# Attention stage of a fused two-block kernel: value products of the local heads turned, the two maps of a differential head joined before their transposes

## What is computed

```python
# local ("swa") heads: 8 query heads of 64, 2 key/value heads, window 128, a sink logit each
p = softmax(concat([scores, sink]))[..., :-1]
y_a = rms_norm(einsum("bnhgqk,bnkhd->bnqhgd", p, vv), swa_out_g)          # over all 512 columns
# differential heads: 4 heads, two maps each, values 128 wide
p_diff = p[:, :, 0] - lam * p[:, :, 1]
y_b = rms_norm(einsum("bhqk,bkhe->bqhe", p_diff, v), subln_g) * (1 - lambda_init)   # per head
x = x + rms_norm(concat([y_a, y_b]) @ w_out, attn_post_g)
```

## Time and profile before

| | |
|---|---|
| median of 3 runs | 759.88 us |
| the profiled execution | 760.85 us |
| its span in the profile | 758.9 us |
| TensorE busy | 749.4 us, 99% |
| VectorE, ScalarE, GpSimd busy | 581.2, 447.7, 211.6 us |
| steps 3 to 22 and the rest of `out2` in the profile | about 388 to 479 us |

### The profile page before, as it was taken

The page is one execution under the profiler, slowest core; times in us unless marked ns, Lnnn a source line. Parts: engine busy times, 40 slices in busy tenths (PEclk is TensorE's granted clock), DMA queues, the critical chain, the costliest instruction groups (busy, mean ns, idle before and its releaser), DMA issues.

```text
span 758.9 us, 16885 instructions
## 1 busy us (share of the span) xinstructions
PE 749.4 (99%) x5994; PEld 728.1 (96%) x5994; DVE 581.2 (77%) x1071; ACT 447.7 (59%) x751; POOL 211.6 (28%) x138
## 2 busy tenths in 40 slices
PE   9999999999999999999999999999999999999997
PEld 8999999999999999999999989999999999988885
DVE  5898986768888877435977896799999999973333
ACT  6644455466665665445855666877666666643431
POOL 0477643460000000342563002522122122122220
PEclk9999999999999999999999999999999999999999
DMA  8565554555555567545443333455555555665651
GB/s 293 191 224 193 184 164 134 195 187 200 188 193 187 177 222 250 189 141 187 141 167 111 114 111 112 139 176 198 196 184 189 193 187 180 214 221 189 183 183 55
DMA packets 37919, 135.49 MB, mean 179 GB/s; under 512 B 4465, under 2 KB 4721, under 8 KB 37873
## 3 DMA queue, kind: packets, MB, share of 16 engines
q1 hardware_dynamic: 37728, 134.86, 53.3%
q10 hardware_dynamic: 144, 0.00, 0.0%
HBM read 133.80 MB, written 1.05 MB: 178 GB/s over the span
## 4 chain that ended last, share of the span: by engine, by line
PE 85%; DVE 5%; ACT 4%; issue 3%; POOL 2%; DMA 1%; DVEq 0%; SPq 0%; POOLq 0%; ACTq 0%
PE bank L1852 24%; PE bank L1853 23%; PE bank L1854 23%; PE bank L2295 4%; PE bank L2294 4%; PE bank L2293 4%; DVE w_lo L1168 2%; ACT w_hi L773 2%; POOL X L741 1%; DMA X<-in_x 1%; PE bank L1908 1%; PE bank L2125 1%; PE bank L2145 0%; ACT score L1063 0%; POOL w_lo L622 0%
## 5 line engine op out<-in xcount | busy, mean ns | idle before, releaser
L1852 PE MATMUL bank<-h_hi,w_hi 128*128 128x256 f32 x1372 | 386.1, 281 | 1.1 <-DVE h_lo L1180 1.0
L1853 PE MATMUL bank<-h_lo,w_hi 128*128 128x256 f32 x1372 | 383.0, 279 | 0.0
L1854 PE MATMUL bank<-h_hi,w_lo 128*128 128x256 f32 x1372 | 383.0, 279 | 0.0
L773 ACT ACTIVATE w_hi<-raw 128x1024 fp32r<-128x1024 f32 (+2 forms) x243 | 258.8, 1067 | 89.9 <-PE bank L2295 41.0
L1168 DVE TENSOR_TENSOR w_lo<-raw,w_hi 128x1024 fp32r<-128x1024 f32 (+2 forms) x187 | 236.1, 1264 | 94.3 <-ACT w_hi L773 92.3
L1852 PEld LDWEIGHTS bank<-h_hi,w_hi 128*128 128x128 f32 x1372 | 257.9, 188 | 2.7 <-DVE w_lo L1246 0.8
L1853 PEld LDWEIGHTS bank<-h_lo,w_hi 128*128 128x128 f32 x1372 | 257.9, 188 | 0.0
L1854 PEld LDWEIGHTS bank<-h_hi,w_lo 128*128 128x128 f32 x1372 | 257.8, 188 | 0.0
L622 POOL TENSOR_TENSOR w_lo<-raw,w_hi 128x1024 fp32r<-128x1024 f32 (+1 forms) x56 | 139.0, 2484 | 380.8 <-ACT w_hi L773 372.6
L1226 DVE TENSOR_TENSOR bank<-bank,scales 128x256 f32<-128x256 f32 x116 | 49.5, 430 | 26.2 <-PE bank L1854 17.6
L1507 DVE SCALAR_TENSOR_TENSOR cg<-bank,vec,cg 128x255 f32<-128x255 f32 x108 | 51.3, 475 | 0.7 <-ACT cg L1003 0.6
(11 more groups left out here) (232 smaller groups left out, 978.8 us busy)
## 6 DMA issues: line engine op xcount, KB each, us to landing
raw<-in_w_up SPq DMA_DIRECT2D x108, 512.0 KB, 3.3
raw<-in_w_in SPq DMA_DIRECT2D x53, 512.0 KB, 3.5
raw<-in_w_down SPq DMA_DIRECT2D x32, 512.0 KB, 4.1
raw<-in_w_down SPq DMA_DIRECT2D x16, 704.0 KB, 4.1
raw<-in_w_o SPq DMA_DIRECT2D x8, 512.0 KB, 3.3
raw<-in_w_gate SPq DMA_DIRECT2D x8, 512.0 KB, 3.4
raw<-in_w_out SPq DMA_DIRECT2D x8, 512.0 KB, 3.3
raw<-in_w_b_out SPq DMA_DIRECT2D x4, 512.0 KB, 3.7
```

Source lines behind the costliest of these rows:

```text
L773: nc.scalar.activation(hi_of(u)[:, cols], raw[s][:, cols], ACT.Copy).then_inc(hi_ready, 1)
L1852: nc.tensor.matmul(ps, wh, hi[:, k, :], start=start and n == 0, stop=False)
L1853: nc.tensor.matmul(ps, wh, lo[:, k, :], start=False, stop=False)
L1854: last = nc.tensor.matmul(ps, wl, hi[:, k, :], start=False, stop=stop and n == len(ks) - 1)
```

## The change

1. **Local heads.** Heads are taken in pairs (one of each key/value group) every second step. v is now the stationary operand, 64 columns wide, and `prob_T` streams, 256 columns and then 128. The outputs of the two heads go to partitions 0 to 63 and 64 to 127, feature-major already. The reciprocals are written 64 times over by VectorE (128x2x64), transposed by TensorE (2), copied by ScalarE (`keep_denominators`), and one VectorE multiply scales the pair (`keep_swa`). The 8 transposes of `y_a` go. Its norm is summed over partitions: ScalarE squares (4), GpSimd adds (3), two 128x1 matmuls (`swa_mean_squares`), mean square, power, two transposes to broadcast (`broadcast_swa_rms`), a ScalarE copy, and VectorE applies gain and scale (`swa_source`, 4).
2. **Differential heads.** GpSimd scales the first map (`scale_first`, 2 instructions), VectorE adds the second map times its own factor (`join`, 2), and one set of transposes and value products per head replaces two. The value product stays in PSUM: squares and scaling read it there.
3. **Order.** The transposes of a joined map come in the step of the second map's reciprocals, behind the scores. In the last step the remaining parts of `out2` units 1 to 3 come ahead of the last transposes of y. Rows of `w_out` and of the gain are permuted on the host.

The core of the diff:

```diff
...
-        steps[m + 3]["score"], steps[m + 4]["trans"], steps[m + 5]["pv"] = m, m, m
+        steps[m + 3]["score"], steps[m + 4]["den"] = m, m
+        if m < N_SWA:
+            steps[m + 4]["trans"] = m
+        if m < N_SWA and m % 2 == 1:
+            steps[m + 5]["swa_pv"] = m // 2
+        if m >= N_SWA and m % 2 == 1:
+            h = (m - N_SWA) // 2
+            steps[m + 4]["trans"], steps[m + 5]["pv"] = N_SWA + h, h
         if m % 2 == 0:
             steps[m + 3]["pair"] = m
-    for i in range(5):
-        at = (7 if i == 0 else 7 + 2 * i) + 5
+    steps[13]["swa_stat"], steps[14]["swa_rms"] = True, True
+    steps[15]["swa_chunks"], steps[16]["swa_chunks"] = [0, 1], [2, 3]
+    for i in range(1, 5):
+        at = 12 + 2 * i
         steps[at]["y_sum"], steps[at + 1]["y_scale"] = i, i
-        steps[at + 2]["y_chunks"] = [0, 1] if i == 0 else [3 + i]
-        if i == 0:
-            steps[at + 3]["y_chunks"] = [2, 3]
+        steps[at + 2]["y_chunks"] = [3 + i]
...
+            def scale_first(m):
+
+                pool.wait_ge(den_done, DEN[m])
+                for b, (lo, hi) in enumerate(block_cols(m)):
+                    nc.gpsimd.tensor_scalar(score[:, m % N_SWA, lo:hi], score[:, m % N_SWA, lo:hi],
+                                            rden[:, m, b:b + 1], None, ALU.mult
+                                            ).then_inc(first_scaled, 1)
...
+                if step["swa_pv"]:
+                    p = step["swa_pv"]
+                    pool.wait_ge(swa_sq, p + 1)
+                    if p > 1:
+                        pool.wait_ge(swa_sum_step, p - 1)
+                    nc.gpsimd.tensor_tensor(swa_sum[:], swa_sq_tile[p][:], swa_sum[:], ALU.add
+                                            ).then_inc(swa_sum_step, 1)
+                if step["swa_rms"] or step["y_scale"] is not None:
+                    i = step["y_scale"] or 0
                     pool.wait_ge(y_ms_done, i + 1)
                     nc.gpsimd.tensor_tensor(y_rstd[:, i, :], y_ms[:, i, :], minus_half[:, 0:2],
                                             ALU.pow).then_inc(y_rstd_done, 1)
+                if step["den"] is not None and step["den"] >= N_SWA and step["den"] % 2 == 0:
+                    scale_first(step["den"])
...
+            def keep_denominators(p):
+
+                act.wait_ge(pv_done, 2 * p + 2)
+                nc.scalar.activation(swa_den[p % 2][:], pv_ps[:, TOK:], ACT.Copy).then_inc(den_kept, 1)
...
             def y_squares(i):
-                act.wait_ge(y_done, 2 * (8 if i == 0 else 8 + 2 * i))
+                act.wait_ge(pv_done, N_SWA + i)
                 for b in range(2):
-                    part = y_a[:, b, :] if i == 0 else y_b[:, b, P * (i - 1):P * i]
-                    if 2 * i + b:
-                        act.wait_ge(y_ss_done, 2 * i + b)
+                    part = pv_ps[:, b * P:(b + 1) * P]
...
+                if step["swa_pv"] is not None:
+                    keep_denominators(step["swa_pv"])
                 if step["trans"] is not None:
                     copy_prob_T(step["trans"])
+                if step["swa_pv"] is not None:
+                    swa_square(step["swa_pv"])
...
+                if kind == "swa":
+                    both = rden_swa[m // 2 % 2][:].rearrange("p (b g n) -> p b g n", b=2, g=2)
+                    nc.vector.reciprocal(both[:, :, h // 4, :], row_sum[:, m, :].unsqueeze(2)
+                                         .broadcast_to([P, 2, HD])).then_inc(den_done, 1)
+                    return
...
+            def join(m):
+
                 dve.wait_ge(den_done, DEN[m])
-                for b in range(2):
-                    if kind == "swa":
-                        nc.vector.tensor_scalar(y_a[:, b, HD * h:HD * (h + 1)],
-                                                pv_ps[:, HD * b:HD * (b + 1)],
-                                                rden[:, m, b:b + 1], None, ALU.mult
-                                                ).then_inc(y_done, 1)
-                    else:
-                        y, pv = y_b[:, b, P * h:P * (h + 1)], pv_ps[:, P * b:P * (b + 1)]
-                        if part == 0:
-                            nc.vector.tensor_scalar(y, pv, rden[:, m, b:b + 1], None, ALU.mult
-                                                    ).then_inc(y_done, 1)
-                        else:
-                            dve.wait_ge(y_done, 2 * m)
-                            nc.vector.scalar_tensor_tensor(y, pv, rden[:, m, b:b + 1], y, ALU.mult,
-                                                           ALU.add).then_inc(y_done, 1)
+                dve.wait_ge(first_scaled, m - N_SWA + 1)
+                for b, (lo, hi) in enumerate(block_cols(m)):
+                    second = score[:, m % N_SWA, lo:hi]
+                    nc.vector.scalar_tensor_tensor(second, second, rden[:, m, b:b + 1],
+                                                   score[:, (m - 1) % N_SWA, lo:hi], ALU.mult, ALU.add
+                                                   ).then_inc(diff_joined, 1)
+
+            def keep_swa(p):
+
+                dve.wait_ge(den_kept, p + 1)
+                nc.vector.tensor_tensor(y_a[:, p, :], pv_ps[:, 0:TOK], swa_den[p % 2][:], ALU.mult
+                                        ).then_inc(y_done, 4)
...
+            def swa_mean_square():
+                dve.wait_ge(swa_stat_done, 1)
+                nc.vector.tensor_scalar(y_ms[:, 0, :], bank[slot(IN2_TILE["swa_stat", 0])][:, 0:2],
+                                        D / 512, EPS, ALU.mult, ALU.add).then_inc(y_ms_done, 1)
+
+            def swa_source(c):
+
+                n = CHUNK0["y"] + c
+                dve.wait_ge(swa_scaled, 1)
+                src_free(n)
+                nc.vector.scalar_tensor_tensor(src[n % 2][:], y_a[:, c, :], vcol("swa_out_g_2", c),
+                                               swa_scales[:], ALU.mult, ALU.mult).then_inc(src_ready, 1)
...
+                if step["swa_rms"]:
+                    swa_mean_square()
+                for c in step["swa_chunks"]:
+                    swa_source(c)
                 if n != LATE_STEP:
                     for c in step["y_chunks"]:
                         y_gained(c)
-                if step["trans"] is not None:
-                    denominators(step["trans"])
-                if step["pv"] is not None:
-                    scaled_output(step["pv"])
+                if step["den"] is not None:
+                    denominators(step["den"])
+                if step["den"] is not None and step["den"] >= N_SWA and step["den"] % 2 == 1:
+                    join(step["den"])
+                if step["swa_pv"] is not None:
+                    keep_swa(step["swa_pv"])
...
             def transposes(m):
-                pe.wait_ge(exp_done, 2 * (m + 1))
-                source = pieces(m)
+                if m < N_SWA:
+                    pe.wait_ge(exp_done, 2 * (m + 1))
+                    source = pieces(m)
+                else:
+                    pe.wait_ge(diff_joined, 2 * (m - N_SWA + 1))
+                    source = pieces(2 * m - N_SWA + 1)
...
-            def value_product(m):
-                kind, h, _ = MAPS[m]
-                width = HD if kind == "swa" else P
-                cols = slice(HD * (h // 4), HD * (h // 4) + HD) if kind == "swa" \
-                    else slice(P * h, P * (h + 1))
-                v = v_a if kind == "swa" else v_b
-                pe.wait_ge(v_ready, 1 if kind == "swa" else h + 2)
-                pe.wait_ge(probT_done, m + 1)
-                if m >= 1:
-                    pe.wait_ge(y_done, 2 * m)
-                pt = prob_T[m % 2]
-                nc.tensor.matmul(pv_ps[:, 0:width], pt[:, 0:P], v[:, 0, cols], start=True, stop=True)
-                nc.tensor.matmul(pv_ps[:, width:2 * width], pt[:, P:2 * P], v[:, 0, cols],
+            def swa_value_products(p):
+
+                pe.wait_ge(v_ready, 1)
+                pe.wait_ge(probT_done, 2 * p + 2)
+                if p >= 1:
+                    pe.wait_ge(y_done, 4 * p)
+                pe.wait_ge(den_done, DEN[2 * p + 1])
+                for b in range(2):
+                    nc.tensor.transpose(pv_ps[:, TOK + b * P:TOK + (b + 1) * P], rden_swa[p % 2][:, b * P:(b + 1) * P],
+                                        ident[:])
+                rows = [slice(HD * g, HD * g + HD) for g in range(2)]
+                for g in range(2):
+                    nc.tensor.matmul(pv_ps[rows[g], 0:TOK], v_a[:, 0, rows[g]], prob_T[g][:, 0:TOK],
+                                     start=True, stop=False)
+                for g in range(2):
+                    nc.tensor.matmul(pv_ps[rows[g], P:TOK], v_a[:, 1, rows[g]],
+                                     prob_T[g][:, 2 * P:3 * P], start=False, stop=True
+                                     ).then_inc(pv_done, 1)
...
+            def broadcast_swa_rms():
+                t = IN2_TILE["swa_rms", 0]
+                bank_free(t)
```

(63 more changed lines are left out.)

69 lines of the change are left out of this document (38 added, 31 removed).

## The result

The changed kernel takes **767.85 us** (median of 6 runs, 766.28 to 768.89) against 760.01 for the kernel before beside it (759.86 to 760.21): a ratio of 1.0097, 95% interval 1.0084 to 1.0110, so 7.8 us slower. The forecast was 763.4 with a range to 767.0: the sign was right, the size was half of it, and the range ended too low.

A forecast was written before the change was run, and what follows sets the result against it. The prediction took TensorE, busy for 99% of the span, to bound the kernel. New waits of 9.3, less 1.7 of old waits and 4.1 of TensorE work, gave +3.5 on 759.88: 763.4 us, range 758.8 to 767.0.

The forecast's parts named there:

- the sum: Whole attention: new waits 9.3, less old waits 1.7, less 4.1 of TensorE work, giving 3.5 us slower.
- a rival at 0.04: TensorE's clock falls to 1.2 GHz behind waits of about 3 us; 2.8 more per projection, 766 or above; chance 0.04.
- steps 17 and 19: TensorE waits at the joined transposes for VectorE's join: 2.8 us in step 17, 3.2 in step 19.
- The waits: TensorE's new waits over the attention, mostly for VectorE's join: 9.3 us in all, against 1.7 before.
- the small ones of the local steps: Steps 7 and 9: ScalarE's added copies and squares make w_hi and exponentials 0.1 late twice, 0.2 us.
- Step 13: Behind the last turned block, a chain of 4.9 us to the join against TensorE's 4.0: wait 0.9.
- the GpSimd rival: Step 13: scale_first stretches beside VectorE's w_lo, ends 0.9 later and delays the join: 764.3; chance 0.10.
- TensorE's own work: TensorE's instructions in the attention: 9.9 us removed, 5.8 added, a fall of 4.1.
- the array rival: Turned local value products: column halves do not overlap, 4 x 0.65 = 2.6 us more, 766.0; chance 0.10.
- The wide reciprocal: VectorE in the local steps: between 0.15 and 1.0 us, covered by idle time; at 1.0 it adds 0.4 in all.
- The faster rival: Joins not held by VectorE's queue, the place being step 17: waits 3.9 in all, 758.0 us; chance 0.15.

The follow-up runs named there:

- the kernel with both fillers: Changed kernel plus idle fp32 matmuls ahead of the joined transposes, 10 in step 17 and 9 in step 19; 764.92 us.
- the differential half alone: Kernel before with only the differential heads changed (joined maps transposed once, behind the scores), local heads as before; 767.67 us.
- `e_late2`: Changed kernel with joined transposes, statistic and broadcast inside the next step's projection, and the copy to prob_T ahead of ScalarE's exponentials; 760.75 us.
- step 17's filler: Changed kernel plus 10 idle fp32 matmuls ahead of the joined transposes of step 17 only; 766.31 us.

## Why the prediction was wrong in size

**The step that failed** is the sum, 9.3 - 1.7 - 4.1 = +3.5: it has no term for what TensorE's clock does behind the waits, which I put into a rival at 0.04 with the words that TensorE never waited over 0.5 so far. The runs showed 3.0 by the rows, and 2.9 by the medians of the kernel with both fillers (2.4 by its trace). Of the 4.3 us that the sum missed these 3.0 are the most, and the waits are 0.8; TensorE's work, half a microsecond lighter than costed, goes the other way. The condition of that rival, waits of about 3 us, was part of my own forecast for steps 17 and 19; a rival whose condition the main case fulfils can't have a twelfth of its chance. The price there, 2.8 more for one projection at half clock, was about right for the pair of falls.

**The waits** were right in place, releaser and nearly in size: 9.5 for the five named against 9.1, and 0.7 for the small ones of the local steps against 0.2. The one of step 19 is in part luck: it was 2.8 because the slow clock brought TensorE there late, and with step 17's wait filled it was 3.4. Step 13 is 0.4 longer than costed, and `scale_first` is part of it. GpSimd and VectorE there:

```profile
428.34 2.23 POOL L734 TENSOR_SCALAR score<-score,rden 128x128 f32<-128x128 f32 x2
```

```profile
428.52 1.26 DVE L1224 TENSOR_TENSOR w_lo<-raw,w_hi 128x1024 fp32r<-128x1024 f32 x1 [0.33 <-ACT w_hi L810]
...
430.22 0.37 DVE L1706 TENSOR_SCALAR rden<-rden,neg_lam 128x2 f32<-128x2 f32 x1
430.69 0.75 DVE L1715 SCALAR_TENSOR_TENSOR score<-score,rden 128x128 f32<-128x128 f32 x2
```

The scaling takes 2.23 beside `w_lo` and 1.53 alone, and ends at 430.57. The join starts 0.47 behind VectorE's instruction on `rden`, where it starts 0.26 behind it in steps 15, 17 and 19. So the GpSimd rival is there, with about 0.2 of its 0.9.

**TensorE's own work** stands as costed within some tenths. A local pair now, TensorE in step 8, answers to the two value products in the earlier trace rows:

```profile
398.68 0.38 PE L2233 MATMUL bank<-ident,tmp 128*128 128x128 f32 x2
398.99 0.65 PE L2237 MATMUL bank<-prob_T,v_a 128*64 128x256 f32 x4
399.47 0.39 PE L2240 MATMUL bank<-prob_T,v_a 128*64 128x128 f32 x4
399.79 0.55 PE L2221 MATMUL bank<-ident,score 128*128 128x128 f32 x3
```

From 398.68 to 399.79 it is 1.11, and about 0.05 more falls on the projection behind; I had 0.22 + 1.07 = 1.29. Halves by columns overlap, as halves by rows do: the array rival is out. Over four pairs that is half a microsecond less than costed. That leaves about 0.6 us of the stage's 7.4 without a place, and the medians lie another 0.4 further apart than the stages of the two traces. Both stay open.

**The wide reciprocal**, which had no row, takes 0.94, near the upper bound of 1.0. It was covered, save for the tenths at steps 7 and 9.

**The faster rival**, joins not held by VectorE's queue, is out: with the queue's order changed the waits fall by 3.7 of 8.6, so the queue did hold them. They fall no further, since the maximum is late on the same engine.

**The earlier evidence** for VectorE as the next bound was in the earlier trace rows: but for the gap of 0.97 it had hardly an idle moment over steps 16 and 17. I used that to price waits, and not to ask what 4 us less on TensorE could bring at all.

## What to carry to other kernels

When a change makes the busiest engine lighter but makes it wait on an engine that is nearly as full over the same steps, price each wait twice: its length, and what the granted clock does behind it. Here 5.9 us of waits at two places cost 2.4 to 2.9 more in slower matmuls, on a page that showed a busy share of 98% and a clock of 9 tenths throughout. Slow matmuls ahead of another wait are partly free, because the wait gets shorter by as much. Moving the waiting instruction later only helps if everything behind it, on every engine, is moved with it in the right order.

## What the runs showed that I had not expected

The length of a wait alone doesn't tell whether the clock falls. With the differential half alone it fell behind a wait of 1.79 in step 13 and not behind one of 2.49 in step 15:

```profile
428.00:431.20 3.20, 1.47 (x14) 1.08 (x12) 1.84 (x8) 1.79 (x7) 0.73 (x1) 1.00 0.51 161
431.20:435.00 3.80, 3.74 (x20) 3.74 (x21) 3.10 (x7) 2.31 (x6) 0.00 (x0) 0.57 0.01 2
440.40:443.80 3.40, 0.97 (x10) 0.70 (x8) 2.75 (x10) 1.72 (x8) 0.74 (x1) 1.00 0.46 154
443.80:447.00 3.20, 3.14 (x27) 3.14 (x28) 3.17 (x9) 2.31 (x6) 0.00 (x0) 1.00 0.00 0
```

In `e_late2` it fell a microsecond after TensorE had started again, at 460.6, behind a wait of 1.74, and not behind one of 2.15 eight microseconds earlier. It also differs from one execution of a kernel to the next, as the mean granted clocks above show: from 0.995 to 0.999 in the four of the kernel with step 17's filler, 0.995 or 0.996 against 0.999 or 1.000 in the eleven of `e_late2`. All six of the changed kernel have 0.995. With the filler the time goes with the clock, in `e_late2` it doesn't. The spread of times alone is no sign of it: 16 executions of the kernel before, whose trace has no fall in the attention, spread over 2.1 us. What decides between two such places, and why the fall cost nothing visible in `e_late2`, was not tried and stays open.
